# Swapping the rotary halves by transfers, and a reciprocal root as exp(-0.5 ln x), in a two-block transformer kernel

## The reference, cut to what matters

```python
def rms_norm(x, g):                       # at each block's start, on heads, on branches, at the end
    y = xf * lax.rsqrt(jnp.mean(xf * xf, axis=-1, keepdims=True) + 1e-6)
    return y * g

def apply_rope(x, cos, sin):              # MLA: q rope parts, one k; SWA: 16 q heads, 4 k heads of 64
    x1, x2 = x[..., :half], x[..., half:] # half = 32
    return concatenate([x1 * cos - x2 * sin, x1 * sin + x2 * cos], axis=-1)
```

## Time and profile before

| what | value |
|---|---|
| three runs | 2753.29, 2753.86 (median), 2761.36 us |
| the profiled execution | 2754.49 us, span of its trace 2752.7 us |
| PE busy | 2655.5 us (96% of the span) |
| DVE busy, ACT busy | 1713.8 us (62%), 1108.0 us (40%) |
| L1185, ACT, high half of a lot | x589, mean 1053 ns |
| L1621, DVE, rest of a lot | x589, mean 1222 ns |
| ACT_TABLE_LOAD | 53 of 1283 ns each, all lines together |
| HBM read | 399.17 MB, 145 GB/s over the span |

### The profile page before, as it was taken

One profiled execution on the slowest core, in us unless ns is written; L12 is line 12 of the kernel. 1 busy time (PEld: TensorE's weight loads), 2 busy tenths in 40 slices (PEclk: granted clock), 3 DMA queues, 4 the chain that ended last, 5 costly groups with the idle time before them and its releaser, 6 DMA issues.

```text
span 2752.7 us, 39891 instructions
## 1 busy us (share of the span) xinstructions
PE 2655.5 (96%) x16424; PEld 2338.3 (85%) x16424; DVE 1713.8 (62%) x2741; ACT 1108.0 (40%) x1745; POOL 0.3 (0%) x5
## 2 busy tenths in 40 slices
PE   6999999999999999999989999999999999998998
PEld 6999899989989998888874688888888888876998
DVE  7566777766768786556651556556665444676655
ACT  5465545545545443322231533223232222355443
POOL 0000000000000000000000000000000000000000
PEclk9999999999999999999999999999999999999999
DMA  4443577634356664445522013445534445331554
GB/s 165 169 143 117 168 234 226 192 130 161 130 168 198 224 214 138 138 149 158 168 69 68 22 65 130 145 152 155 160 121 140 145 150 169 117 115 55 173 180 130
DMA packets 113908, 402.81 MB, mean 146 GB/s; under 512 B 12352, under 2 KB 15552, under 8 KB 113600
## 3 DMA queue, kind: packets, MB, share of 16 engines
q1 hardware_dynamic: 113728, 400.27, 44.9%
HBM read 399.17 MB, written 1.05 MB: 145 GB/s over the span
## 4 chain that ended last, share of the span: by engine, by line
PE 87%; DVE 8%; ACT 3%; issue 1%; DMA 0%; SPq 0%; DVEq 0%; ACTq 0%
PE psum L565 25%; PE psum L566 25%; PE psum L567 25%; PE psum L940 3%; PE psum L974 2%; DVE wlo L1621 1%; ACT whi L1185 1%; DVE R L1662 1%; DVE arena L1662 1%; PE psum L1041 1%; PE psum L1015 1%; DVE arena L1751 1%; PE psum L997 0%; PE psum L985 0%; ACT HHI L1205 0%
## 5 line engine op out<-in xcount | busy, mean ns | idle before, releaser
L565 PE MATMUL psum<-HHI,whi 128*128 128x256 f32 (+1 forms) x3488 | 1121.4, 321 | 34.7 <-DVE wlo L1621 10.9
L566 PE MATMUL psum<-HLO,whi 128*128 128x256 f32 (+1 forms) x3488 | 1107.9, 318 | 0.0
L567 PE MATMUL psum<-HHI,wlo 128*128 128x256 f32 (+1 forms) x3488 | 1107.5, 318 | 0.0
L1621 DVE TENSOR_TENSOR wlo<-wring,whi 128x1024 fp32r<-128x1024 f32 x589 | 706.4, 1222 | 329.8 <-ACT whi L1185 327.6
L1185 ACT ACTIVATE whi<-wring 128x1024 fp32r<-128x1024 f32 x589 | 604.9, 1053 | 384.4 <-PE psum L567 360.8
L565 PEld LDWEIGHTS psum<-HHI,whi 128*128 128x128 f32 x3488 | 671.8, 193 | 90.3 <-issue 16.8
L566 PEld LDWEIGHTS psum<-HLO,whi 128*128 128x128 f32 x3488 | 671.9, 193 | 43.7 <-issue 1.4
L567 PEld LDWEIGHTS psum<-HHI,wlo 128*128 128x128 f32 x3488 | 671.3, 192 | 42.2
L565 PE MATMUL psum<-HIDHI,whi 128*128 128x256 f32 (+1 forms) x1122 | 368.9, 329 | 0.0
L566 PE MATMUL psum<-HIDLO,whi 128*128 128x256 f32 (+1 forms) x1122 | 368.1, 328 | 0.0
L567 PE MATMUL psum<-HIDHI,wlo 128*128 128x256 f32 (+1 forms) x1122 | 368.1, 328 | 0.0
(11 more groups left out here) (301 smaller groups left out, 1984.1 us busy)
## 6 DMA issues: line engine op xcount, KB each, us to landing
wring<-ffn_in SPq DMA_DIRECT2D x264, 512.0 KB, 4.2
wring<-mod_w SPq DMA_DIRECT2D x144, 512.0 KB, 4.3
wring<-ffn_out SPq DMA_DIRECT2D x96, 448.0 KB, 4.0
wring<-w_proj SPq DMA_DIRECT2D x66, 512.0 KB, 4.0
wring<-w_gate SPq DMA_DIRECT2D x64, 512.0 KB, 4.0
wring<-ffn_out SPq DMA_DIRECT2D x48, 512.0 KB, 4.3
wring<-w_up SPq DMA_DIRECT2D x20, 512.0 KB, 3.5
wring<-w_out SPq DMA_DIRECT2D x16, 512.0 KB, 3.5
```

Source lines behind the costliest of these rows:

```text
L565: mm(out_, w[0], a[0], start=start, stop=False)
L566: mm(out_, w[0], a[1], start=False, stop=False)
L567: return mm(out_, w[1], a[0], start=False, stop=stop)
L1621: TTN(wlo[:, i, :], wring[:, raw_slot(tag, k), :], whi[:, i, :].bitcast(F32), ALU.subtract).then_inc(sem("weights_lo"), 1)
```

## The change

1. Each `root` + `invert` becomes `rsqrt` on ACT alone: Ln of mean + eps, then Exp of -0.5 times it. DVE's 26 long reciprocals go. `root_table` becomes `logarithm_table` at the same places, with two new calls.
2. The products with `turn` and the constant go. SP exchanges the 32-row halves by four transfers within SBUF for each step, from its place in the weight stream; the sign moves into `sin2`. In MLA the key's `turn` moves on DVE behind the six scalings of `CQ`.

```diff
+        def swapped(sp, key, dst, src):
+            for a in range(0, P, 32):
+                b = a ^ 32
+                ins = sp.dma_start(dst[a:a + 32], src[b:b + 32])
+                ins.then_inc(*mark(f"swapped_{key}", a // 32, 16))
+
+        def swap_ahead_of(sp, tag, j):
+            if (tag, j) == ("uq", 4):
+                sp.wait_ge(*done("mla_down", 6))
+                swapped(sp, "mla_k", b2["KR"][:, 0, :], b2["KA"][:, 0, 0:SEQ])
+            if (tag, j) == ("mlao", 0):
+                sp.wait_ge(*done("mla_qr", 3))
+                swapped(sp, "mla_q", b2["QX"][:, :, :], b2["QR"][:, :, 0:SEQ])
+            if (tag, j) == ("qkv", 10):
+                sp.wait_ge(*done("swa_kab", 1))
+                swapped(sp, "swa_k", b3["KR"][:, :, :], b3["KAB"][:, :, 0:SEQ])
+            t = j - 10 if tag == "qkv" else j + 2 if tag == "swao" else -1
+            if 0 <= t < 8:
+                sp.wait_ge(*done("swa_qs", t))
+                swapped(sp, f"swa_q{t}", b3["QX"][:, t, :], b3["QS"][:, t, :])
+
         def stream(sp, tag, src, size=None):
             for j in range(LOTS[tag]):
+                swap_ahead_of(sp, tag, j)
                 to_slot(sp, tag, j, src(j), size(j) if size else SLOT)
...
-            def turned(key, event, src):          # and its 15 calls on PE
...
-            def root_table():
-                A(SPARE[:, 0:1], one, ACT.Sqrt)
+            def logarithm_table():
+                A(SPARE[:, 0:1], one, ACT.Ln)
...
                 half_factor(norm, 0)              # in half_tail, ACT
                 half_hi(norm, 0, range(2), l, n3)
                 split_ahead(tag, lots_[0])
+                logarithm_table()
...
-            def root(out_, bank_key, n, count, name, key):
+            def rsqrt(out_, bank_key, n, count, name, key):
                 act.wait_ge(*done("filled", bank_key))
-                A(flat(out_), bank_of(bank_key)[:, 0:n], ACT.Sqrt, bias=eps, scale=1.0 / count).then_inc(*freed(bank_key, name, key))
+                bank = bank_of(bank_key)
+                out_ = flat(out_)
+                A(out_, bank[:, 0:n], ACT.Ln, bias=eps, scale=1.0 / count).then_inc(*freed(bank_key))
+                act.wait_ge(*done("free", bank_key))
+                A(out_, out_, ACT.Exp, scale=-0.5).then_inc(*mark(name, key))
...
                                 half_hi(norm, 1, range(2 * m - 8, 2 * m - 6), 0, 0)   # in ffn, norm ("b0", 0)
+                                if m == 5:
+                                    logarithm_table()
...
-            def invert(buf):                      # and its calls on DVE
-                ln(v.reciprocal(buf, buf))
...
-            def turn(dst, src, key, a, b):
-                v.wait_ge(*done("filled", key))
+            def turn(dst, src, key, a):
+                v.wait_ge(*done(f"swapped_{key}", 3))
                 TTN(a, src, cst("cos2"), ALU.mult)
-                TTN(b, bank_of(key)[:, 0:SEQ], cst("sin2"), ALU.mult).then_inc(*freed(key))
-                v.wait_ge(*done("free", key))
-                return TTN(dst, a, b, ALU.add)
+                ln(TTN(dst, dst, cst("sin2"), ALU.mult))
+                return TTN(dst, a, dst, ALU.add)
```

More of the change, by code:

```diff
@@ L69 @@
 _at = 0
-for _name, _w in (("ident", P), ("ones", P), ("heads64", P), ("turn", P), ("mask_low", P), ("mask_up", P), ("chunk_up", P), ("tri_up", P),
+for _name, _w in (("ident", P), ("ones", P), ("heads64", P), ("mask_low", P), ("mask_up", P), ("chunk_up", P), ("tri_up", P),
                   ("cos2", SEQ), ("sin2", SEQ),
@@ L1199, in half_factor @@
             def half_factor(tag, s_):
-                root(R[:, seqs(s_)], ("ss", tag, s_), SEQ, D, "factor", (tag, s_))
+                rsqrt(R[:, seqs(s_)], ("ss", tag, s_), SEQ, D, "factor", (tag, s_))
             def half_hi(tag, s_, tiles_, l, n3):
@@ L1339, in fox_act @@
                     for i in range(2):
-                        root(t1["RF"][:, 2 * i:2 * i + 2, :], ("ssf", l, i), 512, HD, "fox_r", (l, i))
+                        rsqrt(t1["RF"][:, 2 * i:2 * i + 2, :], ("ssf", l, i), 512, HD, "fox_r", (l, i))
                 if FOX_SCORES <= j < FOX_SCORES + HEADS:
@@ L1381, in gla_act @@
                 gate_step(l, "gss")
-                root(g1["OQ"], ("gss", l), 512, HD, "gla_r", l)
+                rsqrt(g1["OQ"], ("gss", l), 512, HD, "gla_r", l)
             def head_values(l, okey, buf, name):
@@ L1399, in ret_act @@
                 gate_step(l, "rss")
-                root(r1["OQ"], ("rss", l), 512, HD, "ret_r", l)
+                rsqrt(r1["OQ"], ("rss", l), 512, HD, "ret_r", l)
             def ssd_act(l):
@@ L1415, in ssd_act @@
                 gate_step(l, "yss")
-                root(d1["OQ"][:, 0:2, :], ("yss", l), 512, 256, "ssd_r", l)
+                rsqrt(d1["OQ"][:, 0:2, :], ("yss", l), 512, 256, "ssd_r", l)
             def merge_act(l):
@@ L1448, in mla_act @@
                 for part, count in ((0, 512), (1, 256)):
-                    root(b2["RM"][:, part, :], ("mss", part), 512, count, "mla_r", part)
+                    rsqrt(b2["RM"][:, part, :], ("mss", part), 512, count, "mla_r", part)
                 for t in range(12):
@@ L1555, in _ @@
             act.wait_ge(*done("par_loaded", 0))
-            root_table()
+            logarithm_table()
             for k in range(SLOTS):
@@ L1559, in _ @@
             for l in range(DEPTH):
-                root(R[:, 0:SEQ], ("ss", ("n1", l)), SEQ, D, "factor", ("n1", l))
+                rsqrt(R[:, 0:SEQ], ("ss", ("n1", l)), SEQ, D, "factor", ("n1", l))
                 norm_hi(("n1", l), SEQ)
@@ L1571, in _ @@
                 residual(f"wo{l}", ("n2", l), SEQ)
-                root(R[:, 0:SEQ], ("ss", ("n2", l)), SEQ, D, "factor", ("n2", l))
+                rsqrt(R[:, 0:SEQ], ("ss", ("n2", l)), SEQ, D, "factor", ("n2", l))
                 norm_hi(("n2", l), SEQ)
@@ L1584, in _ @@
                 if l:
-                    root(R[:, 0:n], ("ss", ("b2", l)), n, D, "factor", ("b2", l))
+                    rsqrt(R[:, 0:n], ("ss", ("b2", l)), n, D, "factor", ("b2", l))
                     norm_hi(("b2", l), n, l, 2)
                 ffn(f"ffi2{l}1", f"ffo2{l}1", ("b2", l), n, *((("b0", 1), BOTH) if l == 0 else ("final", SEQ)))
-            root(R[:, 0:SEQ], ("ss", "final"), SEQ, D, "factor", "final")
+            rsqrt(R[:, 0:SEQ], ("ss", "final"), SEQ, D, "factor", "final")
         @block.vector
```

42 lines of the change are left out of this document (9 added, 33 removed).

## The result

The changed kernel takes 2733.1 us (median of 4 runs, 2732.7 to 2736.3) against 2755.7 us for the kernel before (4 runs); the ratio is 0.9918, 95% interval 0.9900 to 0.9936. The forecast was 2729. The profiled execution took 2732.96 us (span 2731.2), 21.5 less than that of before (2754.49); the forecast's sum was 25.0.

The account below looks back on a forecast made before the run. TensorE's own work was taken as the bound (87% of the chain of waits), then its waits. Terms from 12.3 us (forgetting attention) down to -0.9 summed to 25.0 us off 2754.49: 2729.5, median forecast 2729, range 2716 to 2742.

Parts of the forecast that it names:

- The price of an rsqrt: Every norm factor: a 1.28 us table load between Ln and Exp; 1.7 us (256 columns) or 1.9 (512) replace the reciprocal.
- rival C: All rsqrt calls: Ln and Exp share a table, no load between; 17 us more gained, 2712 us; chance 0.05.
- rival D: Table loads on the path: each of 21 switches costs its 1.28 us once more, from a drain; 2764 us; chance 0.05.
- Forgetting attention: Both layers: 2.2 us each from earlier operands, plus 7.9 us because the clock no longer falls; 12.3 us gained.
- Rival A: Forgetting attention: the clock still falls there, so 7.9 us are not gained; 2737 us; chance 0.19.
- gla, ssd, norms: Shorter factor chains: gla to ret 2.8 us gained, ssd at the merge 0.4, single norms 2.6 in sum.
- ("b0", 0): Norm where DVE is the bound: 0.7 us won, but an added early table load delays ACT; net 0.8 us lost.
- Half_tails: Four half_tails: the reciprocal's gain is spent on ACT's queue, three also get the 1.5 us preload; 0.8 us lost.
- MLA: MLA's factor: 4.1 us of the 7.5 us wait gained, 0.9 taken back for the clock; query products 1.7 gained.
- SWA: Eight of ten rotary products gone from TensorE, 0.43 us each: 3.4 us gained; first maxima follow as before.
- Rival B: SWA: swaps land late (from about 8 us) and DVE, in order, waits for each; 2737 us; chance 0.08.
- DVE's waits for the swaps under 3 us: Promised sign: DVE waits some 2.5 us for SWA's keys' swap, queued behind a 512 KB load.

Follow-up runs that it names:

- e10: Changed kernel plus two more table switches (an Exp and a Ln of one column) between Ln and Exp of gla's factor, both layers; 2739.8 us.
- e4: Changed kernel with one added 512-column reciprocal delaying DVE behind the wait for the forgetting attention's factor; 2744.4 us.
- e5: Changed kernel without the early logarithm table call at m = 5 of the norm of the second stack; 2730.2 us.
- e3: Changed kernel with root and 1024-column reciprocal back in the forgetting attention alone; 2742.1 us.
- e6: Changed kernel with the forgetting attention's factor as Ln, Ln, then one Exp over both halves; 2729.9 us.
- e8: Changed kernel with the high part of tile 7 ahead of the second factor in the four half tails; 2732.9 us.
- e7: Changed kernel with SWA's last two turns (t = 6, 7) moved behind the first weights; 2730.7 us.
- e9: Changed kernel with each of SWA's eight query swaps issued as eight transfers of half the columns, same bytes; 2752.2 us.
- r1: The changed kernel once more, unchanged; 2733.9 us.

## Why the prediction was right

**The price of an rsqrt** held everywhere: 1.28 us between Ln and Exp, all 28 times, and in MLA from the start of Ln to the first scaling 2.66 us, as forecast. That the two functions share a table (rival C) and that a switch costs double (rival D) are both out, the first by the rows of L1263 and the second by e10. The forecast's "some 26" more loads came out (79 less 53).

The Trainium skill says in "ScalarE: Activation LUTs", section "Table sets: the hidden batching unit", that ln followed by exp takes one load. Here a load stands between them all 28 times; whether another choice of set would save it, no run shows. Its section "What ACT_TABLE_LOAD costs" has about 1283 ns for the load, which stand in every row, and a drain of about 1380 ns besides, which e10's 1.50 us for a whole switch leave no room for.

**Forgetting attention.** 12.6 us against 12.3, the largest term, with the cause shown by e4. The forecast of its pieces holds too: 0.52 us ahead of lot 12 (forecast 0.6), no wait at the scores, clock 1.00. Rival A is out.

**gla, ssd, norms.** 2.9, 0.8 and 1.2 against 2.8, 0.4 and 1.3. L873's wait is 0.40 (promised 0.4).

**("b0", 0).** The wait grew by 0.8 us as forecast, and by the forecast's cause: e5 removes the preload and 1.5 us of wait. What the sum left out is that the clock fell behind the longer wait (3.4 us low, 1.5 lost), though it had weighed just that for MLA. The wait alone does not settle it: with 3.5 us of it 7 of 10 profiles have one (3.4 or 6.8 us; e3, e6 and e8 have none), with 2.0 to 2.7 us 1 of 4.

**Half_tails.** Forecast 0.8 lost, measured 0.7. In three of the four the waits are as long as before in sum, in three pieces of 0.40, 1.39 and 0.49 instead of one of 2.2. In the trace the high part of tile 7 does stand behind load and Exp, and DVE for it:

```profile
1382.61 1.28 ACT L1263 ACT_TABLE_LOAD   x1
1383.91 0.42 ACT L1263 ACTIVATE R<-R 128x256 f32<-128x256 f32 x1
...
1384.23 0.49 ACT L1213 ACTIVATE HHI<-arena,MODS 128x256 fp32r<-128x256 f32 x1
...
1384.75 0.48 DVE L1696 SCALAR_TENSOR_TENSOR HLO<-arena,MODS,HHI 128x256 fp32r<-128x256 f32 x1 [1.88 <-ACT HHI L1213]
```

**MLA.** ACT, DVE and PE after, around the factor, against the earlier trace rows:

```profile
1425.03 0.69 ACT L1261 ACTIVATE arena<-psum,const 128x512 f32<-128x512 f32 x1 [1.54 <-PE psum L981]
...
1427.03 0.63 ACT L1263 ACTIVATE arena<-arena 128x512 f32<-128x512 f32 x1
...
1427.69 2.74 DVE L2170 SCALAR_TENSOR_TENSOR arena<-arena,par 128x512 f32<-128x512 f32 x4 [22.77 <-ACT arena L1263]
...
1430.49 2.43 PE L991 MATMUL psum<-arena,wring 128*128 128x512 f32 x4 [3.78 <-DVE arena L2170]
```

The lead gained is 4.0 us, forecast 4.1. The wait is 3.8 and not the 3.4 that was promised, because PE, without the key's product (0.43 us), arrives at it earlier: what a wait loses and what the place gains are two numbers. The 0.9 us taken back for the clock were nearly not needed (0.1).

**SWA**, the step that failed: "the first maxima follow by ACT's and DVE's halves of the last lot, as before". The products gave 3.8 us where 3.4 was forecast; 2.1 went at once into the wait for the first weights. Of these, 0.9 are PE's, which comes to that wait without the last products, and 1.2 are DVE's: 0.5 for the last swap, and 0.7 for the last lot's halves, which stand behind ACT's high part. ACT in turn waits for weights that SP issued late, behind the swaps: 7.1 us in four waits for `w_swa_o` to land, where before it waits for none of them (the prediction had "only weight loads with four slots in hand" behind the swaps).

```profile
L1193 ACT ACTIVATE whi<-wring 128x1024 fp32r<-128x1024 f32 x589 | 604.9, 1053 | 390.6 <-PE psum L591 362.7 <-DMA wring<-w_swa_o 7.1 <-DMA wring<-ffn_out 5.9
```

e7 shows that DVE's order is what holds the first weights. SP issues a step of four transfers and one of weights in 3.1 us, a little slower than PE takes a lot, so the swaps run late until the end. The prediction bounded the swaps by their landing (3.4 to 9.0 us; 32 KB took 2.8) and counted "11 steps of four transfers" without giving an issue its 0.6 us. Rival B named the regime and set its beginning by the landing; e9 reaches it by the issue. The promised "DVE's waits for the swaps under 3 us" fails with 3.73 in SWA. (In MLA DVE stands 45.9 us ahead of the swapped queries, with nothing else to do; before it stood 52.6 there for the products.)

**The clock elsewhere.** The 6.1 us lost to low stretches at ssd, n2 and ("b0", 0) were not in the sum, and part of what came back behind SWA wasn't either. At ssd it is the same instructions with another length (e7); at ("b0", 0) a longer wait came with it; at n2 the wait was 1.8 us in both kernels, and what differs isn't known. The range of the forecast covered it, the sum did not.

## What to carry to other kernels

A wait of TensorE is worth more than its length where the clock falls behind it: at the attention 2.4 us of waiting taken away brought 5.5 to 7.1. Count each instruction that a queue gets, also the four small transfers that issue in 0.6 us each: here the sum of the issues against the time of a lot decided, not the landing. When an exchange moves work from DVE to ACT, look at what ACT has queued behind it, and put early table loads only where ACT has idle time: one of them cost 1.5 us of waiting.

## What was not expected of the hardware

- The low stretches of these profiles are 3.4, 6.8 or 10.2 us long, in e4, e8 and e9 once 13.7; only the one at the end (10.1 to 11.8) has other lengths. Behind the same small products it is 3.4 or 6.8 us long in kernels with the same code up to there (after and e7), but the same program showed the same lengths in two profiled executions (after and r1).
- In SWA SP takes 0.51 to 0.59 us for nearly every issue within SBUF of 16 or 32 KB (one took 1.43) and 0.58 for most of the 512 KB of weights between them: the size makes no difference. (Loads of weights elsewhere have rows from 0.33 us.)
- Between Ln and Exp stands a table load each time (28 times), 1.283 us, with 0.01 to 0.02 us ahead of it and behind it.
